# Placing the scatter of a pass's right output half behind the next pass's w3 product in a mixer and MoE layer

## What is computed

```python
x = h + grouped_moe(rms_norm(h, norm_ffn_gain), router_w, router_bias, moe_w1, moe_w3, moe_w2)
# in grouped_moe, E = 16 experts, D = 1024, F = 512:
h = silu(einsum('td,edf->tef', xt, w1)) * einsum('td,edf->tef', xt, w3)
h = h * gate[:, :, None]
y = einsum('tef,efd->td', h, w2)
```

## Time and profile before

| | us |
|---|---|
| median of 3 runs | 496.3 (495.28 to 499.4) |
| profiled execution, device time | 496.56 |
| its span | 494.8 |
| PE busy | 474.7 (96%) |
| DVE busy | 238.2 (48%) |
| ACT busy | 176.0 (36%) |
| mean granted TensorE clock | 0.988 of full speed |

### The profile page before, as it was taken

How to read it: one execution, slowest core, us unless ns; L and a number is a source line. 1 busy time by engine, 2 the same in 40 slices (tenths; PEclk the granted TensorE clock), 3 DMA queues, 4 the chain that set the end, 5 groups by cost and what they waited for, 6 DMA issues and landing times.

```text
span 494.8 us, 7869 instructions
## 1 busy us (share of the span) xinstructions
PE 474.7 (96%) x3253; PEld 302.3 (61%) x3253; DVE 238.2 (48%) x395; ACT 176.0 (36%) x263; POOL 6.9 (1%) x19
## 2 busy tenths in 40 slices
PE   6999999999999999999999999999999999998982
PEld 5897998878788888888886434434333343432321
DVE  4858766676657275566367631422215040403034
ACT  5554654685694073435173101201012011200104
POOL 4010000000000000000000000000000000000000
PEclk9999999999999999999998999999999999999998
DMA  8986476431443980948497599999999999999922
GB/s 278 387 263 258 172 289 221 171 115 56 171 170 126 406 320 0 358 152 316 194 356 323 213 424 419 421 357 423 367 425 421 422 424 419 421 421 421 421 83 85
DMA packets 37615, 144.58 MB, mean 292 GB/s; under 512 B 4552, under 2 KB 7248, under 8 KB 25296
## 3 DMA queue, kind: packets, MB, share of 16 engines
q1 hardware_dynamic: 37584, 144.14, 74.3%
HBM read 143.09 MB, written 1.05 MB: 291 GB/s over the span
## 4 chain that ended last, share of the span: by engine, by line
PE 92%; DVE 4%; DMA 2%; ACT 1%; issue 0%; SPq 0%; DVEq 0%; ACTq 0%
PE bank L1719 34%; PE bank L1475 31%; PE bank L1462 11%; PE bank L1730 3%; PE bank L1710 2%; DMA ring<-in_w_in 2%; DVE work L1381 2%; PE bank L1573 1%; PE bank L1790 1%; PE bank L1684 1%; PE bank L1677 1%; DVE x_lo L902 1%; ACT gate L853 1%; PE bank L1560 1%; PE bank L1587 0%; DVE ring_lo L877 0%
## 5 line engine op out<-in xcount | busy, mean ns | idle before, releaser
L1719 PE MATMUL bank<-ring,work 128*32 128x512 f32 x1280 | 141.5, 594 | 2.2 <-ACT work L829 2.2
L877 DVE TENSOR_TENSOR ring_lo<-ring,w_hi 128x2048 fp32r<-128x2048 f32 x38 | 86.3, 2286 | 20.1 <-ACT w_hi L631 20.1
L1719 PEld LDWEIGHTS bank<-ring,work 128*32 128x32 f32 x1280 | 39.7, 110 | 91.0 <-issue 89.0
L631 ACT ACTIVATE w_hi<-ring 128x2048 fp32r<-128x2048 f32 x37 | 70.3, 1910 | 55.1 <-DMA ring<-in_w_in 28.7
L1381 DVE SCALAR_TENSOR_TENSOR work<-bank,st,work 128x512 f32<-128x512 f32 x8 | 8.9, 1118 | 72.9 <-PE bank L1719 72.9
L1475 PE MATMUL bank<-w_hi,x_hi 128*128 128x512 f32 x144 | 39.5, 396 | 0.0
L1475 PE MATMUL bank<-w_hi,x_lo 128*128 128x512 f32 x144 | 38.6, 390 | 0.0
L1475 PE MATMUL bank<-ring_lo,x_hi 128*128 128x512 f32 x144 | 38.6, 390 | 0.0
L1475 PEld LDWEIGHTS bank<-w_hi,x_lo 128*128 128x128 f32 x144 | 27.0, 188 | 5.7
L1475 PEld LDWEIGHTS bank<-ring_lo,x_hi 128*128 128x128 f32 x144 | 27.0, 188 | 5.7
L1364 DVE TENSOR_TENSOR ye_lo<-bank,ye_hi 128x512 fp32r<-128x512 f32 x16 | 11.1, 692 | 40.0 <-ACT ye_hi L809 39.8
(11 more groups left out here) (284 smaller groups left out, 584.6 us busy)
## 6 DMA issues: line engine op xcount, KB each, us to landing
ring<-in_moe_w SPq DMA_DIRECT2D x80, 1024.0 KB, 12.1
ring<-in_w_in SPq DMA_DIRECT2D x13, 2048.0 KB, 9.1
late_slot<-in_moe_w SPq DMA_DIRECT2D x16, 1024.0 KB, 14.8
ring<-in_w_out SPq DMA_DIRECT2D x2, 2048.0 KB, 11.3
ring<-in_w_in SPq DMA_DIRECT2D x2, 1024.0 KB, 10.1
ring<-in_w_up_b SPq DMA_DIRECT2D x1, 2048.0 KB, 8.7
ring<-in_w_up_c SPq DMA_DIRECT2D x1, 2048.0 KB, 7.4
ring<-in_w_up_a SPq DMA_DIRECT2D x1, 2048.0 KB, 9.1
```

Source lines behind the costliest of these rows:

```text
L631: act.activation(hi(q), raw(q), ACT.Copy).then_inc(w_hi_ready, 1)
L877: dve.tensor_tensor(lo(q), raw(q), hi(q).bitcast(F32), ALU.subtract).then_inc(w_lo_ready, 1)
L1719: ins = pe.matmul(bank[cols, dst, :], lhsT[:, k, first + j * STRIP:first + (j + 1) * STRIP], rhs[e][:, k, :], start=(k == 0), stop=(k == n ...
```

## The change

In every pass but (0,0) the scatter of the right half moves on PE from between the w1 and the w3 product to behind the w3 product, ahead of the first gather (in the last round, ahead of the wait for `he`). PE takes the scatter's two waits already ahead of the w3 product, since that product overwrites the bank that the right half was copied from. DVE waits for `he_turned` ahead of `pass_rows`, since `pass_rows` overwrites the `selT` that the moved scatter reads.

```diff
@@ block.vector, expert_pass
                 if y:
                     if not end:
                         gathered_rows(4, fills(m, 1, 0))
+                    dve.wait_ge(he_turned, n + 1)
                     pass_rows(6 * m + 6, 0, True)
                     low_y(4 * m + 3, 0, z3)
...
                 else:
+                    dve.wait_ge(he_turned, n + 1)
                     pass_rows(6 * m + 3, 1, True)
                     low_y(4 * m + 1, 0, z3)
@@ block.tensor, expert_pass
                 ins.then_inc(w1_done, 1)
                 if y or not first:
-                    scatter(4 * m + 2 * y, 1 - y, 1)
+
+                    pe.wait_ge(ye_a, 4 * m + 2 * y)
+                    pe.wait_ge(ye_d, 4 * m + 2 * y)
                 else:
...
                 apart = first and not y
-                if not apart and not end:
-                    next_round(0)
+                if not apart:
+                    scatter(4 * m + 2 * y, 1 - y, 1)
+                    if not end:
+                        next_round(0)
                 pe.wait_ge(he_ready, n + 1)
```

## The result

| | before | after |
|---|---|---|
| median of 6 runs, us | 496.19 (495.28 to 499.4) | 490.99 (490.12 to 491.89) |
| ratio | | 0.988, 95% interval 0.9841 to 0.9919 |
| profiled execution, us | 496.56 | 491.23 |
| its span | 494.8 | 489.5 |
| PE busy | 474.7 | 470.9 |

The changed kernel is faster by 5.2 us, 1.0%, where 3.0 us were forecast (496.3 to 493.3). The time is inside the range given, 490.9 to 496.4, but only 0.1 us from its lower end, and the gain is 1.7 times the forecast. The ratio of 0.988 is that of the means of the six runs, 496.72 and 490.94, which lie 5.8 us apart. Three later executions, of 608.7 to 696.3 us at a mean clock of 0.65 to 0.75, are left out of all figures.

A forecast was written before the change was run, and what follows sets the result against it. PE's issue and short waits bound the kernel, with loads at full DMA rate beside it. PE's 5.65 us is cut by loads at pass (3,0) to 1.9 + 1.2 = 3.1 us, giving a median of 493.3; range 490.9 to 496.4.

The forecast's parts named there:

- The gain on PE: Passes (0,1) to (2,1) gain 0.65 us each, the last round's two 1.2 each: 5.65 us on PE alone.
- The last round's 1.2: In the two last-round passes the scatter fits into PE's idle time, so the whole 1.2 us stays, twice.
- The collision with the loads: At w2 of pass (3,0) PE waits 0.9 and 1.5 us for weights; gain there 1.9 us, not 4.45.
- D: How much earlier the weight loads land by pass (3,0): 1.3 us taken, bounds 0 and 2.4.
- its sum: 1.9 us gained up to w2 of pass (3,0) plus 1.2 in pass (3,1): 3.1 us.
- the hole at 350 us: DMA gap from 349.6 to 352.8 at 215 GB/s, missing 1.56 us of full rate; expected to shrink.
- the first hole: DMA gap from 322.8 to 325.8 at 175 GB/s, missing 1.75 us; its load was to come 0.65 us earlier.
- The added waits: DVE's wait for he_turned and PE's two waits ahead of w3 cost nil; DVE's has 3.8 us slack.
- The rival that was written down: New waits at w2 of (3,0) and (3,1) halve the clock for one stretch, losing 3.4 us: 496.8; chance 0.04.
- The loads do not keep up: Rival judged: landings move as much as PE gains, so the whole 5.65 us arrive: 490.7; chance 0.12.
- The landings do move: Rival judged: landings stay put or the rate is lower; PE gains 0.6 us and the last pass: 494.6; chance 0.14.
- The change does what it says: Rival judged: w3 misses w1's pace or L1381 comes later, so the 1.2 us shrinks: 496; chance 0.08.

The follow-up runs named there:

- c_before: The kernel before, run once more with no edit: median 497.07 us over 12 runs, ratio 0.9994.
- c_after: The changed kernel, run once more with no edit: median 491.09 us over 6 runs, ratio 0.9874 to the kernel before.
- fill_before: The kernel before plus four unread scatter-shaped matmuls in each last-round pass, ahead of the wait for he: median 494.93 us, ratio 0.9945.
- inner_only: Against the kernel before, the scatter moved in passes (0,1) to (2,1) only, DVE's waits added everywhere: median 493.07 us, ratio 0.9911.

## Why the prediction was partly right

**The gain on PE.** Right in kind; the size was a little small. The strips of w1 and w3 run on in one pace: 13.87 us for 128, foretold 13.9. The transposes stand 2.0 us behind the first scatter matmul (415.67 to 417.67) with no wait; in the last round 1.42 us with a wait of 0.21, foretold 0.3 to 0.4. A pass with gathers gained 0.75 where 0.65 was foretold: the chain has w2 of (1,0), (1,1) and (2,0) at 342.72, 368.22 and 393.72, a period of 25.50, against 26.25 before. Most of the tenth is the way from the transposes to w2, 1.48 us (417.67 to 419.15) where it was 1.55 (423.21 to 424.76). The last round's 1.2 held. In all 6.3 us on PE, foretold 5.65.

**The collision with the loads.** Right in the mechanism: the place, both waits (0.8 and 1.3 us; foretold 0.9 and 1.5) and that no earlier pass would wait. Mis-sized was D, the shift of the landings: 1.3 taken, 2.0 measured, from 453.5 − 272.6 = 180.9 behind the first strip to 449.7 − 270.8 = 178.9. With D = 2.0 its sum, 0.7 + 2.0 − 0.1 + 1.2, gives 3.8 for E; the two profiles show 3.9. What PE gained more per pass does not enter there, it only lengthens the waits. The load behind the hole at 350 us is issued 77.2 us behind the first strip in before and 75.7 in after, so the issue gained 1.5 where the prediction had 1.3. The other 0.5 us of D are not explained; they are within that landing's scatter in the six profiles with the old issues (180.4 to 181.3), and between c_before and c_after D is 2.4. The hole itself lost 1.56 us of the full rate before; in the window of the changed kernel over its place, 346.0 to 349.5, (1 − 328/420) × 3.5 = 0.77 is left, so it closed by half:

```profile
346.00:349.50 3.50, 3.50 (x36) 0.91 (x28) 0.69 (x1) 0.60 (x1) 0.00 (x0) 1.00 0.94 328
```

At the landing ahead of the hole the shift was already 1.3 (352.4 − 272.6 against 349.3 − 270.8), and 0.7 between c_before and c_after, where the prediction had 0.65 from the first hole. So how much of D comes from which hole stays open.

**The added waits.** Right inside the passes, nil. Wrong by 0.4 us in the tail.

**The step that failed: the clock of the kernel before.** The prediction made its sum against one profiled execution, read the last round's waits as 1.31 and 0.76 us that "leave the clock at 1.00", and put the clock at nothing in the kernel before. That was true of this execution, but not of most. In the profile of c_before the clock falls behind the same waits, twice, for 3.3 us, and 55 of 88 runs of that kernel have the mean clock that goes with two falls. The rival that was written down had the clock fall after the change. It went the other way: the scatter takes up 1.0 of the 1.38 us of idle time, and no run of after shows both falls. So the kernel before loses 3.3 us in some 6 of 10 executions, 2.1 us in the mean, which the changed one does not. This term was missing from the sum, which took the median and the profiled execution of before for the same thing but for 0.26 us.

**What makes up the 5.2 us.** In each execution the change gives 3.9 us in E, less 0.4 in the tail: 3.5, where the sum had 3.1. The rest of the first measurement can only be estimated, since the clocks of its six runs of before are not on record. Two of them (497.95 and 499.4) lie where all the runs with falls lie, and four (495.28 to 496.3) where all those without do. Without falls the two would be 3.3 us shorter and the median 0.5 lower. The 1.2 us that are then left are most likely chance ahead of the expert part, whose first strip stood at 272.6 and 270.8 in the two profiles. Over many runs the falls weigh more: the mean of the 88 is 497.1 and that of the twelve runs of after and c_after 491.0, 6.1 us apart, of which 3.5 and 2.1 are accounted for. The chance of 0.83 went to a time within 1%, which ended at 491.3; the sum that was 0.4 short and the missing falls carried the time past it. Of the three runs shown at the start, 499.4 lies 3.1 us above the next, and the text used this spread as noise of the loads. It was a sign of two kinds of executions.

**The rivals.** The loads do not keep up: the waits are there. The landings do move. The change does what it says. That the time came near that of the loads keeping up (490.7) is chance; its mechanism is refuted by the two waits on loads.

The Trainium skill (TensorE: Matmul & The Clock Gate, Part 1) has the clock gate follow how busy the array has been; c_before and fill_before agree with it, 1.0 us of filler in each of two passes turning a mean clock of 0.984 into 0.987 and more. A rule on the clock should have been asked of the kernel before too.

## What to carry to other kernels

Moving work into an idle gap of TensorE can pay more than the gap, since the gap may cost clock behind it, as it did in most executions here; look for that in the mean clock of every timed run, not in one profile, and take a spread of the runs' times as a question. Where PE is the bound and loads run at full rate beside it, list for each load when it lands and when it is used: the gain stops at the one with the least slack, and the order in the queue decides which that is. If a change brings PE nearer to its loads, reorder them by first use before anything else; here that was worth another 2.3 us, and nothing without the change.

## What the runs showed of the hardware that was not expected

- The same code, with the same waits of 1.31 and 0.76 us, keeps the full clock in one execution and loses it in another: 214.7 against 211.4 us for E. Each fall lasted 3.4 us. Ahead of the expert part it lasted 3.4 us in some executions and 6.8 in others (257.8 to 264.7 in the earlier trace rows).
- More waiting does not have to cost clock. The changed kernel waits 0.21, 1.58 and 1.32 us in pass (3,0), 3.1 in all where before has 2.1, and its clock stays up there in both profiles.
- Eight filler matmuls in the idle time made the kernel faster, 494.93 against 498.13 us.
- How long the load behind the hole of 350 us takes to land does not follow from how much earlier than the landing ahead of it it is issued. In before it took 6.8 us, issued 2.6 us ahead of that landing (352.4); in after 5.2, issued 2.8 ahead (349.3); in inner_only 6.7, issued 4.2 ahead (345.17 against 349.4).
- More wait instructions in DVE's stream, met or not, cost 0.4 us at a place far behind them.
